# Hybrid decoder layer: the products of the triangular inverse take all 128 columns

## The chip, the cores and the metric

The kernel runs on one core of one Trainium2 chip. The metric is the device time of one execution in microseconds (us), taken as the median of several runs.

## The reference: what is computed

One layer of a decoder trunk, in float32, on 1024 tokens of width 1024: a SwiGLU feed-forward of width 2816, a token mixer, cross-attention over 256 memory tokens, a second SwiGLU. The change lies in the token mixer's first half, RWKV-7:

```python
def step(state, xs):
    r_t, w_t, k_t, v_t, kk_t, b_t = xs
    sa = jnp.einsum('bhvk,bhk->bhv', state, -kk_t)
    state = (state * w_t[:, :, None, :] + sa[..., None] * b_t[:, :, None, :]
             + v_t[..., None] * k_t[:, :, None, :])
    return state, jnp.einsum('bhvk,bhk->bhv', state, r_t)
```

There are 8 heads of width 64. The kernel doesn't walk over the tokens: for each segment of 128 tokens and each head it needs the inverse of a unit lower triangular 128x128 matrix, I + A, where A holds the products of the segment's keys below the diagonal.

## The kernel before

**Stages.** Feed-forward 1, the projections, the mixer (about 1120 to 1740 us of the span), the merge, the attention, feed-forward 2. In the mixer a loop of eight passes (`iteration(i, ...)`, i = 0 to 7, one for each segment) is written out by hand on every engine. Each engine runs its own list in order, and semaphores named after the steps (`W3`, `Wc3`, ...) tie them together.

**The inverse.** It is built by doubling blocks, in six levels n = 1 to 6 with blocks of b = 2^n. `Ur` holds the transposed inverse of the blocks so far for all 8 heads (128 x 8 x 128), `Tr` the inverse not transposed, `AL` the part of A that joins two blocks at this level. One level is this chain:

- TensorE, step W: 8 products (one for each head) of `AL` and `Ur` into PSUM tile g1. The 64 columns used are the odd blocks of `Ur`; the others are left out, so that 8 x 64 columns fill one PSUM bank.
- ScalarE, step Wc (L1450): copies g1 to `Wr`. Behind it, from level 2 on, step Tc (L1458) brings the last level's new half of the inverse into `Tr`, from a transpose made by VectorE (steps T, L1932) or, for the last two levels, by TensorE (step V: `Ur` times an identity into g2).
- TensorE, step E: 8 products of `Tr` and `Wr` into g0. It waits for Tc, at level 1 for Wc.
- VectorE, step U (L1928): subtracts g0 from the odd blocks of `Ur`. The next W waits for it, and for GpSimd's `AL` of its level (L691).

**What lies between.** TensorE fills the waits with other work in a fixed order: the products of the mLSTM half of the mixer, and pieces of the projection of the merge gates (`fill`, L884: 128x512 products of `hq` and `gw`), in slots of a set number (`gates("a4")` stands between W and E of level 4, `gates("b4")` behind E). The slots are the same in passes 1, 2, 4, 5, 6 and 7; pass 3 has none from `a4` on, pass 0 has more of them early.

```python
early = dict(s1=3, s2=2, s3=5, s4=4, s5=4, s6=6)
middle = dict(s7=5, a1=6, b1=4, b2=4, b3=5)
late = dict(a4=4, b4=5, a5=3, b5=4, a6=2, b6=4, F=2)
```

GpSimd makes `AL` of level 4 only after it has finished the output of the pass before (`Ys`, `yo`).

Of the kernel before, what the change touches and what calls it, by code (L numbers as in the profile page):

```python
# [15 lines left out]
P = 128  # L16
# [3 lines left out]
HALF = 512  # L20
# [8 lines left out]
HD = 64  # L29
# [10 lines left out]
LEVELS = 7  # L40
# [11 lines left out]
ACT = mybir.ActivationFunctionType  # L52
F32 = mybir.dt.float32
# [78 lines left out]
def layer_kernel(nc, a, out):  # L132
# [90 lines left out]
    idr = place("mix", "small", "idr", [P, P], F32R)  # L223
# [9 lines left out]
    Ur, Tr = (mix(n, (P, NH, SEG), F32R) for n in ("Ur", "Tr"))  # L233
    levels_at = top["mix"]
    Wr = mix("Wr", (P, NH, SEG), F32R)
# [3 lines left out]
    AL = mix("AL", (P, 2, NH, SEG), F32R)  # L239
# [70 lines left out]
    def flat(ap):  # L310
        return ap.rearrange("p a b -> p (a b)")

    def blocks(ap, n, odd):

        return ap.rearrange("p (q two b) -> p q two b", two=2, b=1 << n)[:, :, odd, :]

    def packed(ap, n):

        return ap.rearrange("p (q b) -> p q b", b=1 << n)

    def con(col, n=P, rows=P):
        return cst[0:rows, col:col + n]
# [428 lines left out]
    def _(pe):  # L751
# [148 lines left out]
        def iteration(i, front, back, more=True):  # L900
            F, B, M = f_pe, b_pe, m_pe
            j = i - 1
            g0, g1, g2, m0, m1 = G[0], G[1], G[2], G[3][:, 0, :], G[3][:, 1, :]
# [22 lines left out]

                fill(slots[min(i, NSEG)].get(slot, 0))

            def level(dst, n, left, right):

                for h in range(NH):
                    last = nc.tensor.matmul(packed(dst[:, 0, h * HD:(h + 1) * HD], n), left[:, h, :], right(h),  # L932
                                            start=True, stop=True)
                return last

            def turned(n):

                return level(g2, n, Ur, lambda h: blocks(idr[:, 0:P], n, 0)).then_inc(*F.sig(f"V{n}"))

            if front:  # L940
                gates("s1")
# [4 lines left out]
            if back:  # L946
# [4 lines left out]
                for n, e, r, rows in heads:  # L951
                    last = nc.tensor.matmul(g2[:, e, r * HD:(r + 1) * HD], W1m[rows, r, :], S0s[rows, r, :],
                                            start=False, stop=r == RC - 1, skip_group_check=True)
                last.then_inc(*B.sig("U"))
            gates("s3" if front else "x1")
            if back:
                pe.wait_ge(*b_act.at("Un", j))
                for n, e, r, rows in heads:
                    nc.tensor.matmul(g2[rows, e, r * P:(r + 1) * P], vtok[:, r, rows], Mv[:, n, :], start=r == 0,
                                     stop=False, skip_group_check=True)  # L960
                for n, e, r, rows in heads:
                    nc.tensor.matmul(g2[rows, e, r * P:(r + 1) * P], Un[:, n, :], Mu[:, n, :], start=False,
                                     stop=False, skip_group_check=True)
                for n, e, r, rows in heads:
                    last = nc.tensor.matmul(g2[rows, e, r * P:(r + 1) * P], S0s[rows, r, :], rho[rows, r, :],
                                            start=False, stop=r == RC - 1, skip_group_check=True)
# [3 lines left out]
                for n, e, r, rows in heads:  # L970
                    nc.tensor.matmul(g1[rows, 1, r * HD:(r + 1) * HD], ktok[:, r, rows], vtok[:, r, rows],
                                     start=r == 0, stop=False, skip_group_check=True)
                for n, e, r, rows in heads:
                    last = nc.tensor.matmul(g1[rows, 1, r * HD:(r + 1) * HD], btok[:, r, rows], Un[:, n, :],
                                            start=False, stop=r == RC - 1, skip_group_check=True)
                last.then_inc(*B.sig("dS"))
            if front:
# [9 lines left out]
                                 stop=True).then_inc(*F.sig("bonus"))  # L987
# [44 lines left out]
            for n in range(1, LEVELS):  # L1032
                pe.wait_ge(*f_dve.at(f"U{n - 1}", i))
                pe.wait_ge(*f_pool.at(f"am{n}", i))
                level(g1, n, AL[:, n % 2], lambda h: blocks(Ur[:, h, :], n, 1)).then_inc(*F.sig(f"W{n}"))
                if n == 1:
                    gates("a1")
                    pe.wait_ge(*f_pool.at("T0", i))
                    pe.wait_ge(*f_dve.at("B", i))
                elif n - 1 > SMALL:  # L1040
                    pe.wait_ge(*f_dve.at("Mv", i))
                    turned(n - 1)
                if n == 2:
                    pe.wait_ge(*m_dve.at("qe", i))
                    nc.tensor.matmul(m0, con(C_ONES), flat(Pb[:]), start=True, stop=False)
                    for h in range(MH):
                        last = nc.tensor.matmul(m0[:, h * SEG:(h + 1) * SEG], CN[:, 1, h, :], qe[:, h, :],
                                                start=False, stop=h == MH - 1)
                    last.then_inc(*M.sig("den"))
                if n == 3:  # L1050
                    pe.wait_ge(*m_act.at("aden", i))
                    for h in range(MH):
                        dst = m0[:, h * SEG:(h + 1) * SEG]
                        nc.tensor.matmul(dst, mvtok[:, h, :], Pb[:, h, :], start=True, stop=False)
                        last = nc.tensor.matmul(dst, CN[:, 0, h, :], qe[:, h, :], start=False, stop=True)
                    last.then_inc(*M.sig("num"))
                if n == 5:
                    pe.wait_ge(*m_dve.at("hm", i))
                    nc.tensor.matmul(m0, con(C_ONES), flat(hm[:]), start=True, stop=True).then_inc(*M.sig("mean"))
                if n == 6:  # L1060
                    pe.wait_ge(*m_pool.at("ysq", i))
                    nc.tensor.matmul(m0, con(C_ONES), flat(mysq[:]), start=True, stop=True).then_inc(*M.sig("var"))
                if n > 1:
                    gates(f"a{n}")
                pe.wait_ge(*f_act.at(f"Wc{n}" if n == 1 else f"Tc{n - 1}", i))
                level(g0, n, Tr, lambda h: packed(flat(Wr[:])[:, h * HD:(h + 1) * HD], n)).then_inc(*F.sig(f"E{n}"))
                if n == 1:
                    pe.wait_ge(*b_dve.at("ve", j))
                    gram(kap, rho, g2).then_inc(*F.sig("Mv"))
                gates(f"b{n}")  # L1070
# [12 lines left out]
            for n, e, r, rows in heads:  # L1083
                last = nc.tensor.matmul(g2[rows, 1, r * P:(r + 1) * P], atok[:, r, rows], Uf[:, n, :],
                                        start=True, stop=True)
# [142 lines left out]
    def _(act):  # L1228
# [166 lines left out]
        def iteration(i, front, back, more=True):  # L1395
# [51 lines left out]
                return  # L1447
            for n in range(1, LEVELS):
                act.wait_ge(*f_pe.at(f"W{n}", i))
                activation(flat(Wr[:])[:, 0:HALF], g1[:, 0, :], ACT.Copy).then_inc(*F.sig(f"Wc{n}"))  # L1450
                if n > 1:
                    if n - 1 > SMALL:
                        act.wait_ge(*f_pe.at(f"V{n - 1}", i))
                        src = packed(g2[:, 0, :], n - 1)
                    else:
                        act.wait_ge(*f_dve.at(f"T{n - 1}", i))
                        src = blocks(flat(Uf[:]), n - 1, 0)
                    activation(blocks(flat(Tr[:]), n - 1, 0), src, ACT.Copy).then_inc(*F.sig(f"Tc{n - 1}"))  # L1458
                if n == 2:
                    act.wait_ge(*m_pe.at("den", i))  # L1460
                    activation(flat(aden[:]), m0, ACT.Abs).then_inc(*M.sig("aden"))
# [4 lines left out]
            if more:  # L1466
                nc.scalar.preload_act_table(ACT.Tanh)
            act.wait_ge(*f_pe.at(f"V{LEVELS - 1}", i))
            activation(blocks(flat(Tr[:]), LEVELS - 1, 0), packed(g2[:, 0, :], LEVELS - 1),
                       ACT.Copy).then_inc(*F.sig(f"Tc{LEVELS - 1}"))  # L1470
            if more:
                ahead(i + 1, gate=False)
# [157 lines left out]
    def _(dve):  # L1630
# [181 lines left out]
        def iteration(i, front, back):  # L1812
# [103 lines left out]
            for n in range(1, LEVELS):  # L1916
                if n == 3:
                    dve.wait_ge(*m_act.at("aden", i))
                    tt(aden[:], aden[:], nmb[:], ALU.max).then_inc(*M.sig("dmax"))
                    dve.wait_ge(*M.at("dmax", i))  # L1920
                    nc.vector.reciprocal(aden[:, 0:2], aden[:, 0:2]).then_inc(*M.sig("rec0"))
                if n == 4:
                    nc.vector.reciprocal(aden[:, 2:MH], aden[:, 2:MH]).then_inc(*M.sig("rec"))
                    dve.wait_ge(*M.at("rec", i))
                    dve.wait_ge(*m_pe.at("num", i))
                    tt(flat(hm[:]), m0, flat(aden[:]), ALU.mult).then_inc(*M.sig("hm"))
                dve.wait_ge(*f_pe.at(f"E{n}", i))
                tt(blocks(flat(Ur[:]), n, 1), blocks(flat(Ur[:]).bitcast(F32), n, 1), packed(g0[:, 0, :], n),  # L1928
                   ALU.subtract).then_inc(*F.sig(f"U{n}"))
                if n <= SMALL:  # L1930
                    dve.wait_ge(*F.at(f"U{n}", i))
                    nc.vector.transpose(flat(Uf[:]), flat(Ur[:]).bitcast(F32)).then_inc(*F.sig(f"T{n}"))  # L1932
                if n == 1:
                    dve.wait_ge(*b_dve.at("S", j))
                    dve.wait_ge(*f_pe.at("Mv", i))
                    tt(S0s[:], St[:], Pi[:, :, 0:1].to_broadcast([P, RC, HD]), ALU.mult).then_inc(*F.sig("S0s"))
                    gram("Mv", Mv, g2, C_UPEQ)
                    if back:
                        output_norm()
                if n == 3:  # L1940
                    gate_half(1)
                if n == 5:
                    dve.wait_ge(*m_pe.at("mean", i))
                    stt(flat(hm[:]), m0, -1.0 / P, flat(hm[:]), ALU.mult, ALU.add).then_inc(*M.sig("yc"))
# [251 lines left out]
```

## Time and profile before

| | |
|---|---|
| median of 3 runs | 2991.3 us (2990.96 to 2994.0) |
| time of the profiled execution | 3002.78 us |
| its span, first to last instruction | 3001.0 us |
| TensorE busy | 2877.7 us, 96% |
| VectorE, ScalarE, GpSimd busy | 1353.9, 544.8, 1246.4 us |
| mean granted TensorE clock | 0.975 of full speed |

Full speed is 2.4 GHz, and the profile knows one lower level, 1.2 GHz (0.50). The profile shows TensorE's weight loads (PEld) apart from its products (PE), and a busy PE is not PE at its peak: a product of few columns counts as busy while the next weights are loaded. What matters for a wait in the mixer is whether TensorE stands still for it.

### The profile page before, as it was taken

To read this page: it belongs to the slowest core of one execution; us is meant where nothing else is said; L and a number is where in the kernel's file an instruction comes from. 1 tells how busy PE (TensorE), PEld (TensorE's weight loads), DVE (VectorE), ACT (ScalarE), POOL (GpSimd) and SP (SyncE) were. 2 spreads that over 40 slices of the span, in tenths; PEclk is the share of its full clock that TensorE was granted. 3 is DMA by queue.
4 is the path that set the end of the run, shared out by engine and by line. 5 is a ranking of instruction groups with operands and counts; after the bars stand their busy time and mean duration, and the time that the engine had idled before them with its cause. 6 is when DMAs were issued, how large, how long until landed. Compare 5 with 4: busy or idle time off the path is not lost.

```text
span 3001.0 us, 36791 instructions
## 1 busy us (share of the span) xinstructions
PE 2877.7 (96%) x14694; PEld 2387.5 (80%) x14694; DVE 1353.9 (45%) x1109; ACT 544.8 (18%) x793; POOL 1246.4 (42%) x627
## 2 busy tenths in 40 slices
PE   7999999999999979999999999998899999999996
PEld 6888888888788867777877778888788888888885
DVE  5431331235557525666776645443354321331334
ACT  3100000002001112333433322214311100000011
POOL 3444333334794623555554533331044333334432
PEclk9999999999999999988998999999999999999998
DMA  3111111112862643324442254113011111111111
GB/s 133 47 45 48 49 49 49 49 44 104 320 226 98 233 151 129 94 85 151 99 103 89 82 200 161 49 56 126 0 49 42 49 49 49 49 49 49 49 40 72
DMA packets 115401, 271.35 MB, mean 90 GB/s; under 512 B 7644, under 2 KB 58972, under 8 KB 108272
## 3 DMA queue, kind: packets, MB, share of 16 engines
q1 hardware_dynamic: 93504, 210.79, 21.7%
q10 hardware_dynamic: 21808, 59.27, 5.2%
q8 instruction: 68, 1.11, 0.2%
q14 instruction: 21, 0.17, 0.0%
HBM read 207.56 MB, written 62.44 MB: 90 GB/s over the span
## 4 chain that ended last, share of the span: by engine, by line
PE 78%; issue 9%; POOL 6%; DVE 4%; ACT 1%; DMA 0%; SPq 0%; ACTq 0%; POOLq 0%; DVEq 0%
PE G L760 23%; PE G L762 23%; PE G L761 23%; PE G L884 2%; POOL AL L691 2%; PE G L932 1%; PE G L1173 1%; POOL Tr L685 1%; ACT sx L1567 0%; DVE nt_a L1652 0%; DVE px L2024 0%; DVE mx L2016 0%; POOL rho L674 0%; PE G L1165 0%; SPq L559 0%
## 5 line engine op out<-in xcount | busy, mean ns | idle before, releaser
L724 POOL TENSOR_TENSOR whi<-raw,zero 128x1024 fp32r<-128x1024 f32 (+1 forms) x199 | 378.2, 1900 | 1313.0 <-PE G L762 1233.1
L760 PE MATMUL G<-hhi,whi 128*128 128x512 f32 x2032 | 794.6, 391 | 19.6 <-DVE hlo L1658 16.4
L761 PE MATMUL G<-hlo,whi 128*128 128x512 f32 x2032 | 792.6, 390 | 0.0
L762 PE MATMUL G<-hhi,wlo 128*128 128x512 f32 x2032 | 792.4, 390 | 0.0
L727 POOL TENSOR_TENSOR wlo<-raw,whi 128x1024 fp32r<-128x1024 f32 (+1 forms) x199 | 482.5, 2425 | 15.6
L760 PEld LDWEIGHTS G<-hhi,whi 128*128 128x128 f32 x2032 | 382.7, 188 | 102.5 <-issue 13.1
L761 PEld LDWEIGHTS G<-hlo,whi 128*128 128x128 f32 x2032 | 382.7, 188 | 80.0 <-issue 0.7
L762 PEld LDWEIGHTS G<-hhi,wlo 128*128 128x128 f32 x2032 | 382.8, 188 | 79.5
L760 PE MATMUL G<-ahi,whi 128*128 128x512 f32 x960 | 374.2, 390 | 2.7 <-DVEq L461 2.7
L762 PE MATMUL G<-ahi,wlo 128*128 128x512 f32 x960 | 373.5, 389 | 0.0
L761 PE MATMUL G<-alo,whi 128*128 128x512 f32 x960 | 373.5, 389 | 0.0
L884 PE MATMUL G<-hq,gw 128*128 128x512 f32 x768 | 237.6, 444 | 21.9 <-DVE ev L1810 20.4
L760 PEld LDWEIGHTS G<-ahi,whi 128*128 128x128 f32 x960 | 180.2, 188 | 40.4 <-issue 3.1
L761 PEld LDWEIGHTS G<-alo,whi 128*128 128x128 f32 x960 | 180.2, 188 | 37.5 <-issue 0.2
L762 PEld LDWEIGHTS G<-ahi,wlo 128*128 128x128 f32 x960 | 180.2, 188 | 37.5
L884 PEld LDWEIGHTS G<-hq,gw 128*128 128x128 f32 x768 | 145.4, 203 | 64.5 <-issue 40.1
L1304 ACT ACTIVATE s<-s 128x1024 f32<-128x1024 f32 x44 | 46.7, 1061 | 759.9 <-DVE s L1731 759.9
L1689 DVE SCALAR_TENSOR_TENSOR xT<-G,xT 128x1024 f32 x32 | 39.2, 1225 | 292.2 <-PE G L762 292.2
L1731 DVE TENSOR_TENSOR s<-G,nrx 128x1024 f32<-128x1024 f32 x44 | 53.9, 1225 | 245.8 <-PE G L762 244.9
L1737 DVE TENSOR_TENSOR s<-s,G 128x1024 f32<-128x1024 f32 x44 | 53.8, 1222 | 224.6 <-PE G L762 224.0
L1733 DVE TENSOR_TENSOR s<-s,nrx 128x1024 f32<-128x1024 f32 x44 | 132.6, 3014 | 49.6 <-ACT s L1304 49.6
L1739 DVE TENSOR_TENSOR alo<-s,ahi 128x1024 f32 x44 | 127.5, 2897 | 59.6 <-ACT ahi L1306 59.6
(329 smaller groups left out, 3321.4 us busy)
## 6 DMA issues: line engine op xcount, KB each, us to landing
gw<-gw_d SPq DMA_DIRECT2D x32, 1024.0 KB, 5.4
raw<-in_wg SPq DMA_DIRECT2D x44, 512.0 KB, 3.3
raw<-in_wu SPq DMA_DIRECT2D x44, 512.0 KB, 3.3
raw<-in_wd SPq DMA_DIRECT2D x32, 512.0 KB, 3.3
gw_d<-gw SPq DMA_DIRECT2D x16, 1024.0 KB, 4.7
graw<-in_gates_in SPq DMA_DIRECT2D x16, 512.0 KB, 7.0
raw<-in_ml_in SPq DMA_DIRECT2D x16, 512.0 KB, 3.8
zml_d<-po ACTq DMA_DIRECT2D x16, 512.0 KB, 2.6
```

Source lines behind the costliest of these rows:

```text
L691: tt(AL[:, n % 2], Am[:], copies(C_LEV + n * P), ALU.mult).then_inc(*F.sig(f"am{n}"))
L724: nc.gpsimd.tensor_tensor(whi[:, k, 0:w], raw[:, k, 0:w], zero[:].to_broadcast([P, w]), ALU.add).then_inc(hi_made, 1)
L727: nc.gpsimd.tensor_tensor(wlo[:, k, 0:w], raw[:, k, 0:w], whi[:, k, 0:w].bitcast(F32), ALU.subtract).then_inc(split_made, 1)
L760: nc.tensor.matmul(dst, wh, hi, start=start, stop=False)
L761: nc.tensor.matmul(dst, wh, lo, start=False, stop=False)
L762: return nc.tensor.matmul(dst, wl, hi, start=False, stop=stop)
L884: last = nc.tensor.matmul(G[3][:, 1, :], gw[:, k, way == 2, t * P:(t + 1) * P], hq[:, t + (way == 1) * KD, :], start=at == 0, stop=at == 3 ...
L1304: activation(s0[:], s0[:], ACT.Silu).then_inc(f_silu, 1)
L1731: tt(s0[:], flat(bank_act(c.act + r)[:]), nrx[:], ALU.mult).then_inc(act_free, 1)
L1733: tt(s0[:], s0[:], nrx[:], ALU.mult).then_inc(f_scaled, 1)
L1737: tt(s1[:], s0[:], flat(bank_dve(c.dve + r)[:]), ALU.mult).then_inc(dve_free, 1)
L1739: tt(alo[:, i * 2 + r, :], s1[:], ahi[:, i * 2 + r, :].bitcast(F32), ALU.subtract).then_inc(a_lo, 1)
```

## The change

All three kinds of products take 128 columns for each head: W multiplies by the whole of `Ur`, E by the whole of `Wr`, V by the whole identity. Each fills two PSUM banks in place of one. The number of products stays. Step Wc copies both banks, 1024 elements of a partition in place of 512. Steps U and Tc still handle 512 elements, and now pick the blocks they need out of PSUM with a stride, where PSUM had them packed before.

```diff
-            def level(dst, n, left, right):
+            def turned(n):
 
                 for h in range(NH):
-                    last = nc.tensor.matmul(packed(dst[:, 0, h * HD:(h + 1) * HD], n), left[:, h, :], right(h),
-                                            start=True, stop=True)
-                return last
-
-            def turned(n):
-
-                return level(g2, n, Ur, lambda h: blocks(idr[:, 0:P], n, 0)).then_inc(*F.sig(f"V{n}"))
+                    last = nc.tensor.matmul(flat(g2[:])[:, h * P:(h + 1) * P], Ur[:, h, :], idr[:, 0:P], start=True,
+                                            stop=True)
+                return last.then_inc(*F.sig(f"V{n}"))
...
-                level(g1, n, AL[:, n % 2], lambda h: blocks(Ur[:, h, :], n, 1)).then_inc(*F.sig(f"W{n}"))
+                eight(g1, AL[:, n % 2], Ur).then_inc(*F.sig(f"W{n}"))
...
-                level(g0, n, Tr, lambda h: packed(flat(Wr[:])[:, h * HD:(h + 1) * HD], n)).then_inc(*F.sig(f"E{n}"))
+                eight(g0, Tr, Wr).then_inc(*F.sig(f"E{n}"))
...
-                activation(flat(Wr[:])[:, 0:HALF], g1[:, 0, :], ACT.Copy).then_inc(*F.sig(f"Wc{n}"))
+                activation(flat(Wr[:]), flat(g1[:]), ACT.Copy).then_inc(*F.sig(f"Wc{n}"))
...
-                        src = packed(g2[:, 0, :], n - 1)
+                        src = blocks(flat(g2[:]), n - 1, 0)
...
-            activation(blocks(flat(Tr[:]), LEVELS - 1, 0), packed(g2[:, 0, :], LEVELS - 1),
+            activation(blocks(flat(Tr[:]), LEVELS - 1, 0), blocks(flat(g2[:]), LEVELS - 1, 0),
...
-                tt(blocks(flat(Ur[:]), n, 1), blocks(flat(Ur[:]).bitcast(F32), n, 1), packed(g0[:, 0, :], n),
+                tt(blocks(flat(Ur[:]), n, 1), blocks(flat(Ur[:]).bitcast(F32), n, 1), blocks(flat(g0[:]), n, 1),
```

`eight` was there before:

```python
def eight(dst, left, right):
    for n in range(NH):
        last = nc.tensor.matmul(flat(dst[:])[:, n * P:(n + 1) * P], left[:, n, :], right[:, n, :],
                                start=True, stop=True)
    return last
```

## Rows read from the trace of the kernel before

**Rows 1.** The page: busy times, and the granted clock in 40 slices.

```profile
PE 2877.7 (96%) x14694; PEld 2387.5 (80%) x14694; DVE 1353.9 (45%) x1109; ACT 544.8 (18%) x793; POOL 1246.4 (42%) x627
...
PEclk9999999999999999988998999999999999999998
```

**Rows 2.** Groups by line and shape, 1150 to 1720 us: busy us, mean ns, idle before.

```profile
L932 PE MATMUL G<-Wr,Tr 128*128 128x64 f32 x384 | 56.5, 295 | 3.9 <-ACT Tr L1458 2.4 <-issue 1.5
L932 PE MATMUL G<-Ur,AL 128*128 128x64 f32 x384 | 56.1, 295 | 13.9 <-DVE Uf L1932 6.9 <-POOL AL L691 3.7 <-DVE Ur L1928 3.3
...
L1450 ACT ACTIVATE Wr<-G 128x512 fp32r<-128x512 f32 x48 | 28.7, 598 | 208.3 <-PE G L932 208.3
...
L932 PE MATMUL G<-idr,Ur 128*128 128x64 f32 x128 | 19.5, 301 | 0.0
```

**Rows 3.** Timeline of TensorE, end of pass 0: start us, length us, instructions.

```profile
1192.15 1.99 PE L921 MATMUL G<-Ur,Am 128*128 128x128 f32 x16
1193.89 1.06 PE L932 MATMUL G<-idr,Ur 128*128 128x64 f32 x8
```

**Rows 4.** ScalarE in the attention: its copy of 1024 elements out of PSUM.

```profile
L1563 ACT ACTIVATE pxt<-G 128x1024 f32<-128x1024 f32 x8 | 8.2, 1023 | 7.1 <-PE G L1165 7.1
```

**Rows 5.** Timeline of pass 4, end of level 3 and level 4.

```profile
1472.58 2.38 POOL L691 TENSOR_TENSOR AL<-Am,cst 128x1024 fp32r<-128x1024 f32 x1
...
1472.72 1.41 PE L884 MATMUL G<-hq,gw 128*128 128x512 f32 x5
...
1475.11 1.05 PE L932 MATMUL G<-Ur,AL 128*128 128x64 f32 x8 [0.98 <-DVE Uf L1932]
...
1476.00 1.18 PE L884 MATMUL G<-hq,gw 128*128 128x512 f32 x4
1476.20 0.60 ACT L1450 ACTIVATE Wr<-G 128x512 fp32r<-128x512 f32 x1 [4.84 <-PE G L932]
1476.69 0.62 ACT L1458 ACTIVATE Tr<-Uf 128x512 fp32r<-128x512 f32 x1
...
1477.37 0.85 PE L932 MATMUL G<-Wr,Tr 128*128 128x64 f32 x6 [0.19 <-ACT Tr L1458]
```

**Rows 6.** The same timeline, pass 4, level 2: Tc and E.

```profile
1465.76 0.68 ACT L1458 ACTIVATE Tr<-Uf 128x512 fp32r<-128x512 f32 x1
...
1466.82 1.06 PE L932 MATMUL G<-Wr,Tr 128*128 128x64 f32 x8
```

**Rows 7.** Timeline, pass 4, level 5: Tc and E.

```profile
1481.03 0.62 ACT L1458 ACTIVATE Tr<-Uf 128x512 fp32r<-128x512 f32 x1
...
1481.97 0.97 PE L932 MATMUL G<-Wr,Tr 128*128 128x64 f32 x8
```

**Rows 8.** Timeline of ScalarE: the first Wc of pass 4 and of pass 5.

```profile
1459.99 0.60 ACT L1450 ACTIVATE Wr<-G 128x512 fp32r<-128x512 f32 x1 [4.13 <-PE G L932]
...
1528.98 0.60 ACT L1450 ACTIVATE Wr<-G 128x512 fp32r<-128x512 f32 x1 [4.12 <-PE G L932]
```

**Rows 9.** The same: the first Wc of pass 6 and of pass 7.

```profile
1601.21 0.60 ACT L1450 ACTIVATE Wr<-G 128x512 fp32r<-128x512 f32 x1 [4.11 <-PE G L932]
...
1681.17 0.60 ACT L1450 ACTIVATE Wr<-G 128x512 fp32r<-128x512 f32 x1 [4.12 <-PE G L932]
```

**Rows 10.** Stretches with busy us of each engine, granted clock, DMA share, GB/s.

```profile
1403.90:1421.00 17.10, 15.54 (x61) 13.16 (x60) 3.57 (x5) 4.85 (x7) 6.50 (x5) 0.50 0.61 244
1547.30:1554.10 6.80, 6.80 (x20) 5.09 (x20) 1.94 (x2) 1.11 (x2) 3.22 (x2) 0.50 0.12 48
1619.00:1642.90 23.90, 23.90 (x84) 20.09 (x84) 4.83 (x7) 4.85 (x7) 8.66 (x6) 0.50 0.05 19
1460.00:1528.90 68.90, 65.53 (x535) 54.15 (x535) 51.06 (x64) 26.96 (x53) 38.80 (x25) 1.00 0.46 105
1601.20:1619.00 17.80, 16.36 (x117) 13.72 (x116) 15.80 (x18) 4.60 (x8) 12.86 (x8) 1.00 0.53 156
1165.00:1171.80 6.80, 6.80 (x25) 5.47 (x23) 2.18 (x3) 1.29 (x3) 2.35 (x1) 0.50 0.22 54
```

More of the change, by code:

```diff
@@ L315, in blocks @@
         return ap.rearrange("p (q two b) -> p q two b", two=2, b=1 << n)[:, :, odd, :]
-    def packed(ap, n):
-        return ap.rearrange("p (q b) -> p q b", b=1 << n)
     def con(col, n=P, rows=P):
```

## The prediction

> **What bounds the kernel now.** I read the page first, then the groups of the mixer, then the timeline of one level of the inverse, then the granted clock in stretches. TensorE is busy 96% of the span, and its clock is below full speed in a few slices only, most of them in the mixer [rows 1]. So time goes or comes in three ways: TensorE's own work gets longer, TensorE waits more or less for the chain W, Wc, Tc, E, U, or its clock changes. ScalarE and VectorE are mostly idle; what they do matters only where TensorE has run out of other work.
>
> The chain seldom stops TensorE. Over 48 levels its products waited 3.9 us before E and 13.9 us before W [rows 2]. Level 4 shows both: after five gate products TensorE stands about 1 us until W of level 4, since GpSimd's AL ends only at 1472.58 + 2.38 = 1474.96, and the four gate products behind W end before Tc does, so E waits another 0.19 us [rows 5].
>
> **The products: 112 groups of eight (48 W, 48 E, 16 V), from 64 to 128 columns.** The sixteen records of F, 128 columns each, take 1.99 us from the first start to the last end, eight of 64 columns take 1.06 [rows 3]: eight more in 0.93 us, 0.116 us for each. Within the 64-column group it is (1.06 - 0.30) / 7 = 0.109, taking the last one's length as 0.30 [rows 2]. Both walk at the pace of the weight loads, 128 columns for each product, which don't change. The difference of 0.007 times 896 products is 6.3 us at most; at least it is 0. The tail is the uncertain part of the subtraction, and the pace of the loads explains both numbers, so I take 0.
>
> The Trainium skill (TensorE: Matmul & The Clock Gate, Back-to-back issue gap) gives an isolated gap that grows with the columns, about 60 cycles at 64 and 134 at 128. By it the sum would rise by some 31 ns for each of 896 products, an estimate of 28 us. The rows on F and V speak against that here, because a weight load stands before every product.
>
> **Wc copies 1024 elements.** It takes 0.598 us [rows 2]; ScalarE's copy of 1024 out of PSUM takes 1.023 us [rows 4]. So each Wc ends 0.43 us later, and Tc behind it too. What hides this is the work TensorE has between W and E. Level by level, in a pass at full clock:
>
> - Level 4: Tc ends at 1476.69 + 0.62 = 1477.31, E starts at 1477.37 [rows 5]. No cover: the whole 0.43 us, in the seven passes 1 to 7 (pass 0 has cover), 3.0 us.
> - Level 5: Tc ends at 1481.65, E starts at 1481.97 [rows 7]. Of the 0.32 us some 0.05 is the way from one engine to the other, as at level 4, so 0.27 covers and 0.16 shows; in seven passes 1.1 us. In pass 3, which has no gate products there, up to 0.4 us.
> - Level 2: Tc ends at 1466.44, E starts at 1466.82 [rows 6]; 0.10 us shows. It is absorbed before W of level 4, which waits for GpSimd and not for this chain.
> - Levels 1 and 3 have more cover than level 2. At level 6 Tc waits for V behind W, and that hides Wc.
>
> The sum is +4.5 us. Everything behind U in a pass follows it, so I take nothing as given back. The bounds are 0 and 48 x 0.43 = 20.6 us, the second if nothing covered.
>
> **Strided reads from PSUM in U and Tc.** No row shows a fine stride out of PSUM. The nearest is Tc of level 1's blocks out of SBUF, two elements at a time: 0.68 us against 0.62 at wide blocks [rows 5, 6]. I take 0, as VectorE and ScalarE already step through SBUF in the same pattern; the upper bound is 0.06 x 64 = 3.8 us.
>
> **The clock.** This is the largest term. Pass 4 ran wholly at 2.4 GHz [rows 10], and from its first Wc to that of pass 5 it took 68.99 us [rows 8]. Pass 5 has the same work, contained one stretch of 6.8 us at 1.2 GHz [rows 10], and took 1601.21 - 1528.98 = 72.23 [rows 8, 9], +3.2. Pass 6 contained one of 23.9 us and took 79.96 [rows 9], +11.0. Passes 1 and 2 repeat these two almost to the digit, so there are four such stretches, 28.4 us together. Pass 3 loses its clock for 17.1 us, and pass 0 for 6.8 [rows 10].
>
> Where does it fall? Pass 4's E of level 4 starts 17.38 us after its first Wc [rows 5, 8]. The same offset gives 1546.36 in pass 5 and 1618.59 in pass 6. The clock falls at 1547.3 and 1619.0: 0.9 and 0.4 us later, right behind W, four gate products and E of level 4 with their two waits. At 1601.2 to 1619.0 it was still 1.00 [rows 10]. Passes 4 and 7 have the same place and keep the clock. So this place is marginal: a little less or more work there decides in some passes. After the change the two groups of products there, 16 in all, stream 2048 columns instead of 1024, against 2048 of the four gate products; it is a third more work between the same waits, less what 0.43 us more of waiting before E takes away. And once the clock is low, the following products are wider too, so the long stretch of pass 6 should shrink to the short one.
>
> I price it so. In the profiled execution all four stretches go, 28.4 us, and pass 0's 3.2 too, since it begins behind E of level 1 with the same products. Pass 3 keeps its own: without gate products TensorE really stands still. A remaining fall in one pass of eight or so costs 2.4 us. In this execution's own time: 3002.8 + 4.5 - 31.6 + 2.4 = 2978.
>
> The median before is 2991.3, 11.5 below this execution. I read that as fewer or shorter falls in those runs: 28.4 - 11.5 = 16.9 us are left to win, and for pass 0 on average 1. So 2991.3 + 4.5 - 16.9 - 1.0 + 2.4 = 2980.3. Were the 11.5 us a cost of profiling alone, it would be 2991.3 + 4.5 - 31.6 + 2.4 = 2967, the lower end.
>
> **The rivals.**
>
> *The clock doesn't care for columns.* The records call TensorE just as busy with 64 columns as with 128: a busy share can't tell them apart. Then only the ScalarE term stays: 2991.3 + 4.5 = 2995.8, within what can be told from no change (0.2%, 6 us, is about what a measurement of this kernel resolves). For it speaks that passes 4 and 7 keep the clock with the same work, so chance has a part; against it, that the falls stand behind the narrowest work of the pass.
>
> *Slower: the longer wait before E of level 4 pulls the clock down.* E waits 0.19 us now and would wait 0.62. If only standing still counts, passes that now keep the clock lose it. One more long stretch costs 11.0 us [rows 8, 9]: 2995.8 + 11.0 = 3007. It decides as soon as the stretches added cost over 1.5 us, which one short stretch of 3.2 us does.
>
> The Trainium skill (the same page, The HAM clock gate) says that the clock follows how busy the array has been. If busy means occupied, as the records count it, this rival follows. If it means columns streamed, my forecast does. The page doesn't say which, so it gets no more weight than the trace gives it.
>
> *Products at 128 columns cost more than weight loads hide.* At the bound of 6.3 us, plus strided reads at 3.8, the gain shrinks to about nothing: 2980.3 + 10.1 = 2990.4, no change.
>
> **How the numbers follow.** Falls at level 4 mostly vanish: 0.64, 2980, own range 2970 to 2988. Clock unmoved: 0.17, 2996. Products and reads at their bounds: 0.08, 2990. Slower by the clock: 0.11, 3007. The range 2967 to 2997 reaches from profiling as the whole difference to the unmoved clock and leaves out the slower rival and tails, somewhat under 2 in 10. Faster than 2985.3: nearly all of the first case and a little of the third, 0.65. Within 0.2%: 0.22. Slower than 2997.3: 0.13.
>
> **What would show each step.** Right: the 896 products keep a mean near 280 to 295 ns, eight of them still take about 1.06 us; Wc takes 1.02 us; E of level 4 starts 0.43 us later after W than now; U stays at 0.68 us; passes 1, 2, 5 and 6 take 69.5 to 70 us from first Wc to first Wc, and the stretches at 0.50 between 1225 and 1700 us are down to pass 3's and perhaps a short one. Wrong: if passes without a low stretch take over 71 us, the ScalarE or product term was too small. If the low stretches are as many and as long as before, the clock doesn't follow columns. If pass 4 or 7 has one, the second rival holds. If the median falls by less than 6 us though the stretches are gone, the runs before had fewer of them than the difference of 11.5 us made me think.

## The result and the profile after

The changed kernel takes 2977.85 us (median of 5 runs, 2975.95 to 2980.32) against 2994.0 for the kernel before in the same rounds (5 runs, 2990.96 to 2999.85): a ratio of 0.9944, with a 95% interval of 0.9931 to 0.9957. Its profiled execution took 2978.5 us over a span of 2976.7.

The page of the changed kernel, busy times and granted clock, against [rows 1]:

```profile
PE 2850.4 (96%) x14694; PEld 2361.4 (79%) x14694; DVE 1354.5 (46%) x1109; ACT 564.4 (19%) x793; POOL 1247.0 (42%) x627
...
PEclk9999999999999999998999999999999999999998
```

TensorE is busy 27.3 us less, though 896 of its products became twice as wide. ScalarE is busy 19.6 us more. The clock row has one slice under 9 inside the mixer, where it had three.

The groups of the mixer after, 1150 to 1700 us (busy us, mean ns, idle before), against [rows 2]:

```profile
L917 PE MATMUL G<-Wr,Tr 128*128 128x128 f32 x384 | 55.0, 288 | 7.3 <-ACT Tr L1450 5.6 <-DVE Bm L1817 1.5
L917 PE MATMUL G<-Ur,AL 128*128 128x128 f32 x384 | 52.5, 281 | 12.6 <-DVE Uf L1924 6.6 <-POOL AL L687 3.7 <-DVE Ur L1920 1.6
...
L1442 ACT ACTIVATE Wr<-G 128x1024 fp32r<-128x1024 f32 x48 | 49.2, 1025 | 182.2 <-PE G L917 182.2
L1920 DVE TENSOR_TENSOR Ur<-Ur,G 128x512 fp32r<-128x512 f32 x48 | 32.5, 678 | 80.1 <-PE G L917 80.1
...
L928 PE MATMUL G<-idr,Ur 128*128 128x128 f32 x128 | 18.0, 286 | 0.0
```

The wide products have a lower mean (281 to 288 ns) than the narrow ones had (295 to 301), because fewer of them ran at the low clock: in pass 4, at full clock in both kernels, the narrow ones have a mean of 272 to 277 ns and the wide ones 275 to 277. Wc takes 1.025 us. The subtraction U, which now reads PSUM with a stride, takes 0.678 us. Before E, TensorE waits 7.3 us in all in place of 3.9; of it 5.6 are for Tc, where it was 2.4.

Level 4 of pass 4 in the timeline of the changed kernel, against [rows 5]:

```profile
1457.85 2.38 POOL L687 TENSOR_TENSOR AL<-Am,cst 128x1024 fp32r<-128x1024 f32 x1
...
1458.07 1.36 PE L880 MATMUL G<-hq,gw 128*128 128x512 f32 x5
...
1460.38 1.08 PE L917 MATMUL G<-Ur,AL 128*128 128x128 f32 x8 [0.95 <-DVE Uf L1924]
...
1461.29 1.14 PE L880 MATMUL G<-hq,gw 128*128 128x512 f32 x4
1461.49 1.03 ACT L1442 ACTIVATE Wr<-G 128x1024 fp32r<-128x1024 f32 x1 [4.42 <-PE G L917]
...
1462.42 0.62 ACT L1450 ACTIVATE Tr<-Uf 128x512 fp32r<-128x512 f32 x1
...
1463.09 1.11 PE L917 MATMUL G<-Wr,Tr 128*128 128x128 f32 x8 [0.66 <-ACT Tr L1450]
```

From W to E it is 2.71 us in place of 2.26: the 0.43 us of the longer copy and little else. W itself takes 1.08 us for eight products of 128 columns, where it took 1.05 for eight of 64.

The first Wc of passes 4 to 7 in the timeline of ScalarE, against [rows 8, 9]:

```profile
1445.20 1.03 ACT L1442 ACTIVATE Wr<-G 128x1024 fp32r<-128x1024 f32 x1 [4.14 <-PE G L917]
...
1515.07 1.03 ACT L1442 ACTIVATE Wr<-G 128x1024 fp32r<-128x1024 f32 x1 [4.16 <-PE G L917]
...
1584.97 1.03 ACT L1442 ACTIVATE Wr<-G 128x1024 fp32r<-128x1024 f32 x1 [4.14 <-PE G L917]
...
1654.84 1.03 ACT L1442 ACTIVATE Wr<-G 128x1024 fp32r<-128x1024 f32 x1 [4.15 <-PE G L917]
```

The differences are 69.87, 69.90 and 69.87 us, where they were 68.99, 72.23 and 79.96. A pass at full clock has become 0.88 us longer, and now all of them but pass 3 are at full clock. The stretches of the changed kernel (columns as in [rows 10]):

```profile
1225.00:1386.60 161.60, 151.35 (x1210) 124.38 (x1208) 121.99 (x147) 65.12 (x115) 94.73 (x58) 1.00 0.44 112
1386.60:1407.10 20.50, 17.53 (x65) 14.54 (x66) 5.35 (x8) 6.02 (x9) 8.20 (x5) 0.50 0.65 256
1407.20:1690.30 283.10, 266.70 (x2156) 219.05 (x2155) 206.06 (x253) 117.55 (x213) 155.15 (x96) 1.00 0.33 93
1690.40:1700.60 10.20, 10.01 (x54) 9.68 (x55) 4.10 (x7) 1.79 (x3) 3.31 (x3) 0.50 0.41 145
```

Between 1225 and 1690 us only pass 3's stretch, 20.5 us, is left at half clock. The stretch at 1690.4 stands at the end of the mixer, behind level 6 of pass 7; the kernel before has one of 6.8 us there, at 1718.0, so the change doesn't remove it.

### The profile page after: what moved, and what is told of

It is laid out like the page before. It is cut to its first block, busy times and chain, and to the rows that moved or that the text cites. A ratio compares the mean times of both kernels' runs of the same rounds, so it can differ in the third digit from the quotient of the medians.

```text
span 2976.7 us, 36791 instructions
## 1 busy us (share of the span) xinstructions
PE 2850.4 (96%) x14694; PEld 2361.4 (79%) x14694; DVE 1354.5 (46%) x1109; ACT 564.4 (19%) x793; POOL 1247.0 (42%) x627
## 4 chain that ended last, share of the span: by engine, by line
PE 78%; issue 9%; POOL 6%; DVE 4%; ACT 1%; DMA 1%; SPq 0%; POOLq 0%; ACTq 0%; DVEq 0%
PE G L756 24%; PE G L758 24%; PE G L757 24%; PE G L880 2%; POOL AL L687 2%; PE G L1165 1%; PE G L917 1%; POOL Tr L681 1%; ACT sx L1559 0%; DVE nt_a L1644 0%; DVE px L2016 0%; DVE mx L2008 0%; POOL rho L670 0%; PE G L1157 0%; SPq L555 0%
## 5 line engine op out<-in xcount | busy, mean ns | idle before, releaser
L880 PE MATMUL G<-hq,gw 128*128 128x512 f32 x768 | 221.7, 421 | 22.2 <-DVE ev L1802 20.5
L880 PEld LDWEIGHTS G<-hq,gw 128*128 128x128 f32 x768 | 137.8, 192 | 60.1 <-issue 37.0
L1681 DVE SCALAR_TENSOR_TENSOR xT<-G,xT 128x1024 f32 x32 | 39.2, 1225 | 292.2 <-PE G L758 292.2
L1723 DVE TENSOR_TENSOR s<-G,nrx 128x1024 f32<-128x1024 f32 x44 | 53.9, 1225 | 245.8 <-PE G L758 244.9
```

Of the source, the lines that this page charges most:

```text
L880: last = nc.tensor.matmul(G[3][:, 1, :], gw[:, k, way == 2, t * P:(t + 1) * P], hq[:, t + (way == 1) * KD, :], start=at == 0, stop=at == 3 ...
L1723: tt(s0[:], flat(bank_act(c.act + r)[:]), nrx[:], ALU.mult).then_inc(act_free, 1)
```

## Experiments

The main theory is that the gain is the clock, kept up where the wider products stream more columns, and the price is ScalarE's longer copy. The main rivals: the gain comes from the shift in time that the longer copy makes, and waits alone decide over the clock. The kernel before ran beside each group: 2991.8 us in 23 runs beside the first four, 2991.9 in 12 beside the others. "A pass" is the distance between the first Wc of two passes in the profiled execution; "low" counts the stretches at half clock that begin around E of level 4, in the six passes that have gate products there (1, 2, 4, 5, 6 and 7).

| kernel | median us | ratio to before (95% interval) | pass at full clock | low |
|---|---|---|---|---|
| before | 2991.8 | | 68.99 | 4 of 6 |
| changed, again | 2976.9 | 0.9942 (0.9923 to 0.9962) | 69.87 | 0 |
| only W wide | 2969.4 | 0.9922 (0.9901 to 0.9943) | 69.02 | 0 |
| all wide, copy of 512 | 2970.4 | 0.9924 (0.9902 to 0.9945) | 69.14 | 0 |
| all narrow, copy of 1024 | 3005.5 | 1.0046 (1.0028 to 1.0065) | 69.69 | 3 of 6 |
| changed, a4 behind E | 2993.2 | 1.0003 (0.9990 to 1.0016) | none | 6 of 6 |
| all narrow, six gate products in a4 | 2971.5 | 0.9930 (0.9908 to 0.9952) | 68.87 | 0 |
| only E wide | 2971.5 | 0.9935 (0.9909 to 0.9961) | 69.21 | 2 of 6 |
| only W wide, pass 3 filled | 2965.6 | 0.9909 (0.9887 to 0.9930) | 69.02 | 0 |

The profiled execution of the first result has 0 of 6 as well. So at this place the two kernels with narrow products and four gate products before E fell in 7 of 12 passes. The seven executions with more columns there (the changed kernel twice, the four other variants with wide products and four gate products before E, and the narrow one with six) fell in 2 of 42.

### Only W at 128 columns

```diff
-                level(g1, n, AL[:, n % 2], lambda h: blocks(Ur[:, h, :], n, 1)).then_inc(*F.sig(f"W{n}"))
+                eight(g1, AL[:, n % 2], Ur).then_inc(*F.sig(f"W{n}"))
...
-                activation(flat(Wr[:])[:, 0:HALF], g1[:, 0, :], ACT.Copy).then_inc(*F.sig(f"Wc{n}"))
+                activation(packed(flat(Wr[:])[:, 0:HALF], n), blocks(flat(g1[:]), n, 1), ACT.Copy).then_inc(*F.sig(f"Wc{n}"))
```

> The kernel before, with only step W at 128 columns; ScalarE picks the 512 odd elements of a partition out of PSUM with a stride, E and V stay at 64 columns. Half of the added columns, no longer copy. If the clock is kept by the columns streamed behind the wait of level 4, most low stretches of passes 1, 2, 5, 6 go, none of the ScalarE cost (0.88 us a pass in the changed kernel) comes, and it takes 2970 to 2980 us. If the columns are not the cause, it stays at the kernel before, 2990 to 3000, low stretches included. If a strided read out of PSUM costs 0.06 us each or more, passes at full clock take over 69.4 us in place of 69.0.

It took 2969.4 us, 22 below the kernel before and just under the range. The stretches of its trace, and its Wc:

```profile
1225.00:1385.80 160.80, 150.74 (x1217) 125.11 (x1216) 122.85 (x149) 59.51 (x116) 95.68 (x58) 1.00 0.42 115
1385.80:1406.30 20.50, 18.16 (x72) 15.64 (x72) 5.58 (x8) 4.85 (x7) 9.09 (x6) 0.50 0.60 241
1406.40:1686.00 279.60, 263.60 (x2147) 218.12 (x2146) 205.61 (x253) 107.86 (x212) 153.72 (x94) 1.00 0.36 94
...
L1450 ACT ACTIVATE Wr<-G 128x512 fp32r<-128x512 f32 x48 | 28.7, 598 | 190.9 <-PE G L921 190.9
```

A full-clock pass is as long as before (69.02 against 68.99), so there is no gain in the work itself: the same count of instructions, and at level 4 the same waits (1.01 and 0.22 us in pass 4). Pass 6 took 70.81 us without a low stretch, since TensorE stood 1.6 us once before E of level 1 with no release that the profile shows; that is no part of the change. The columns of the 48 groups of W differ, and with them the order in which W reads `Ur` and writes PSUM; the low stretches of passes 1, 2, 5 and 6 are gone. Wc takes 598 ns with the strided read from PSUM, exactly as without it.

### All products wide, ScalarE copies only what is needed

```diff
-                activation(flat(Wr[:]), flat(g1[:]), ACT.Copy).then_inc(*F.sig(f"Wc{n}"))
+                if n == 1:
+                    activation(flat(Wr[:]), flat(g1[:]), ACT.Copy).then_inc(*F.sig(f"Wc{n}"))
+                else:
+                    activation(blocks(flat(Wr[:]), n, 1), blocks(flat(g1[:]), n, 1),
+                               ACT.Copy).then_inc(*F.sig(f"Wc{n}"))
```

> The changed kernel, but from level 2 on ScalarE copies only the odd blocks, 512 elements of a partition, in place; the other columns of Wr keep old numbers that no later step uses. All products at 128 columns, the copy back at about 0.60 us. If the columns hold the clock and the longer copy is the cost, passes at full clock take 69.0 to 69.3 us in place of 69.87, low stretches as few as in the changed kernel, and the time is 5 to 7 us below it: 2971 to 2973. If the longer copy itself had a part in the gain (by moving the passes against the chip's clock control), it is above the changed kernel: 2980 to 2995.

It took 2970.4 us, just under the range and 7.5 below the changed kernel's first result (6.5 below its repeat), and a pass is 69.14 us against its 69.87. So 0.73 of the 0.88 us a pass is the copy, and 0.15 is left for the wider products and the rest, the long copy of level 1 among it. Its two forms of Wc:

```profile
L1445 ACT ACTIVATE Wr<-G 128x512 fp32r<-128x512 f32 x40 | 23.9, 598 | 151.2 <-PE G L917 151.2
L1443 ACT ACTIVATE Wr<-G 128x1024 fp32r<-128x1024 f32 x8 | 8.2, 1029 | 37.4 <-PE G L917 37.4
```

### Only the longer copy, products at 64 columns

```diff
-                activation(flat(Wr[:])[:, 0:HALF], g1[:, 0, :], ACT.Copy).then_inc(*F.sig(f"Wc{n}"))
+                activation(flat(Wr[:]), flat(g1[:]), ACT.Copy).then_inc(*F.sig(f"Wc{n}"))
```

> The kernel before with 64-column products, where only ScalarE's copy Wc takes 1024 elements, the second half being numbers that nothing uses. It has the cost and not the columns. If the columns hold the clock: low stretches as in the kernel before or more, passes at full clock near 69.6 to 69.9 us, and 4 to 15 us slower than before: 2998 to 3009. If the gain came from the longer copy's shift of the passes in time, it is as fast as the changed kernel, 2975 to 2985.

It took 3005.5 us (12 runs, 2995.2 to 3014.8), 13.7 above the kernel before. That the copy's shift in time makes the gain is ruled out. A full-clock pass is 69.69 us, +0.70, or 4.9 us in seven passes. The other 8.8 us I put down to the clock, and the runs agree: their mean clock was 0.971 to 0.978, that of the kernel before beside them 0.975 to 0.982. The profiled execution's level 4 in pass 1, and two of its low stretches:

```profile
1247.03 1.05 PE L932 MATMUL G<-Ur,AL 128*128 128x64 f32 x8 [0.97 <-DVE Uf L1932]
...
1247.91 1.18 PE L884 MATMUL G<-hq,gw 128*128 128x512 f32 x4
1248.11 1.03 ACT L1450 ACTIVATE Wr<-G 128x1024 fp32r<-128x1024 f32 x1 [4.42 <-PE G L932]
...
1249.71 1.91 PE L932 MATMUL G<-Wr,Tr 128*128 128x64 f32 x8 [0.62 <-ACT Tr L1458]
...
1249.60:1273.50 23.90, 23.79 (x81) 19.99 (x82) 4.88 (x7) 5.76 (x8) 8.00 (x5) 0.50 0.06 21
...
1618.20:1625.00 6.80, 6.80 (x21) 5.09 (x21) 2.36 (x3) 1.54 (x2) 2.74 (x2) 0.50 0.15 57
```

The waits (0.97 and 0.62 us) are those of the changed kernel (0.95 and 0.66), the gate products too. Here the clock falls at this very place, 0.1 us before E starts; there it doesn't. Falls came in passes 1, 6 and 7. The copy alone doesn't decide each time: passes 2, 4 and 5 of this execution kept the clock.

### The gate products of a4 moved behind E

```diff
-        late = dict(a4=4, b4=5, a5=3, b5=4, a6=2, b6=4, F=2)
+        late = dict(a4=0, b4=9, a5=3, b5=4, a6=2, b6=4, F=2)
```

> The changed kernel with the four gate products between W and E of level 4 moved behind E (slot a4 from 4 to 0, b4 from 5 to 9). TensorE then stands still for some 1.5 us before E, in each of the passes 0 to 7 that has late slots. By the waits alone it costs about 0.9 us a pass, 6.5 us: 2984. If this place with its work and waits decides over the clock, the low stretches come back in most passes, 3.2 to 11 us each: 3000 to 3040. If the place has nothing to do with it, 2984.

It took 2993.2 us, 15 to 16 above the changed kernel, so all of its gain is lost. Every pass now has a low stretch. Two of its windows, and level 4 of pass 4:

```profile
1249.90:1253.30 3.40, 3.40 (x10) 2.78 (x10) 1.93 (x2) 0.00 (x0) 2.68 (x2) 0.54 0.08 31
1321.60:1328.40 6.80, 6.80 (x26) 5.93 (x25) 1.94 (x2) 0.00 (x0) 3.33 (x2) 0.52 0.16 60
...
1466.22 1.08 PE L917 MATMUL G<-Ur,AL 128*128 128x128 f32 x8 [0.96 <-DVE Uf L1924]
1468.93 1.97 PE L917 MATMUL G<-Wr,Tr 128*128 128x128 f32 x8 [1.63 <-ACT Tr L1450]
```

The stretches are short (3.4 and 6.8 us, and 13.7 in pass 3, which has no gate products there). Nine gate products follow at once; that they shorten the stretches is likely, but not shown. The direction was as expected; the size was below the 3000 to 3040 I gave, since I had priced in long stretches. No pass ran at full clock, so waits and clock can't be split here.

### The marginal place filled another way: six gate products before E, all products narrow

```diff
-        late = dict(a4=4, b4=5, a5=3, b5=4, a6=2, b6=4, F=2)
+        late = dict(a4=6, b4=3, a5=3, b5=4, a6=2, b6=4, F=2)
```

> The kernel before, all products at 64 columns, with two of the gate products behind E of level 4 moved in front of it (slot a4 from 4 to 6, b4 from 5 to 3). At the marginal place this adds 1024 columns, as many as the change does, by another way. If the columns streamed there decide, the low stretches of the passes mostly go though no product is wider, at a cost of about 0.2 us a pass: 2973 to 2983. If the width of the products itself is what matters, it stays at 2990 to 2996.

2971.5 us, just under the range: the kernel before with two numbers of a table changed is faster than the changed kernel. Its passes take 68.87 us, since the wait before E of level 4 is filled, and its stretches are:

```profile
1225.00:1383.00 158.00, 148.66 (x1204) 123.23 (x1202) 120.39 (x146) 58.59 (x114) 93.17 (x57) 1.00 0.40 114
1383.20:1403.60 20.40, 17.92 (x71) 15.40 (x71) 5.33 (x8) 4.94 (x8) 8.82 (x6) 0.51 0.63 253
1406.70:1410.10 3.40, 3.40 (x31) 2.85 (x27) 3.30 (x5) 2.34 (x9) 0.00 (x0) 0.51 0.02 5
1410.60:1683.00 272.40, 259.02 (x2099) 214.11 (x2098) 199.93 (x247) 104.09 (x200) 153.49 (x94) 1.00 0.35 96
```

Both low stretches are pass 3's; the kernel before has the same pair, 17.1 us at 1403.9 and 3.4 at 1424.4.

So the width of the products isn't needed. The pass has no column more than before, two gate products only stand in front of E and not behind it; so the place counts. This run can't take apart how much the columns do and how much the filled wait of 0.19 us. The first experiment keeps that wait and loses the stretches too, but changes the order of W's reads and writes, which this one leaves as it was. What both have in common is more columns at this place.

### Only E at 128 columns

```diff
-                level(g0, n, Tr, lambda h: packed(flat(Wr[:])[:, h * HD:(h + 1) * HD], n)).then_inc(*F.sig(f"E{n}"))
+                eight(g0, Tr, Wr).then_inc(*F.sig(f"E{n}"))
...
-                activation(flat(Wr[:])[:, 0:HALF], g1[:, 0, :], ACT.Copy).then_inc(*F.sig(f"Wc{n}"))
+                if n == 1:
+                    activation(blocks(flat(Wr[:]), n, 0), packed(g1[:, 0, :], n), ACT.Copy)
+                activation(blocks(flat(Wr[:]), n, 1), packed(g1[:, 0, :], n), ACT.Copy).then_inc(*F.sig(f"Wc{n}"))
...
-                tt(blocks(flat(Ur[:]), n, 1), blocks(flat(Ur[:]).bitcast(F32), n, 1), packed(g0[:, 0, :], n),
+                tt(blocks(flat(Ur[:]), n, 1), blocks(flat(Ur[:]).bitcast(F32), n, 1), blocks(flat(g0[:]), n, 1),
```

> The kernel before with only step E at 128 columns: ScalarE spreads the 512 packed elements to the odd blocks of Wr (at level 1 it fills the even ones too, one more copy), U reads PSUM with a stride, W and V stay at 64. Added columns as in the first experiment, but behind the wait. If the columns of either group serve, 2968 to 2978. If only those of W do, since the clock falls behind W and the wait for E, the low stretches stay in part: 2982 to 2995.

2971.5 us (6 runs, 2968.2 to 2984.6), as expected if either group serves. In the profiled execution it serves not quite as well as W: two short stretches of 3.4 us are left at level 4, in passes 5 and 7, where the kernel with W wide has none. That is one execution of each. The slowest run, at a clock of 0.981, may have had more:

```profile
1387.80:1404.80 17.00, 15.44 (x60) 12.95 (x59) 3.44 (x5) 4.85 (x7) 6.30 (x5) 0.50 0.60 241
1412.00:1531.00 119.00, 112.96 (x931) 92.94 (x931) 91.54 (x113) 46.87 (x89) 68.41 (x43) 1.00 0.42 108
1531.20:1534.60 3.40, 3.40 (x13) 2.92 (x13) 1.95 (x3) 0.00 (x0) 3.40 (x2) 0.52 0.27 104
1671.00:1674.40 3.40, 3.40 (x13) 2.92 (x13) 2.15 (x3) 0.00 (x0) 3.40 (x2) 0.50 0.35 135
```

### Pass 3 filled with products that nothing uses

The kernel with only W wide, and in pass 3 thirteen products on constants (the expectation says fourteen) in its empty late slots:

```diff
+                if i == GATES // 4 - 1 and slot in late:
+                    pe.wait_ge(ev_made, made[0] // (3 * KD) + 1)
+                    for _ in range((late[slot] + 1) // 2):
+                        nc.tensor.matmul(G[3][:, 1, 0:2 * P], con(C_ID), con(C_LEV, 2 * P), start=True, stop=True)
```

> The kernel of the first experiment (only W at 128 columns), and in pass 3, whose late slots are empty, half as many float32 products of 256 constant columns as other passes have gate products there; their result is used by nothing. 14 added products of about 0.43 us. If pass 3 loses its clock because TensorE streams too little there, the 20.5 us stretch at 1.2 GHz goes and pass 3 takes about 69 to 70 us in place of 75.5, so 5 to 6 us less in all: about 2964. If the clock falls there for another reason, the 14 products come on top: 2973 to 2976.

It took 2965.6 us, the fastest of all and 26 below the kernel before, with 13 products more than needed; TensorE is busy with them for 7.1 us. Pass 3 takes 68.92 us in place of 75.46. The stretch around it:

```profile
1366.00:1436.00 70.00, 66.63 (x545) 55.72 (x544) 51.30 (x63) 27.80 (x54) 39.97 (x25) 1.00 0.46 154
```

The products fill a wait as well: TensorE stands 0.29 us before E of level 4 in pass 3, where it stood 1.20. This run doesn't tell whether their columns or the shorter wait keep the clock.

### The changed kernel again

> The changed kernel again, so that it stands beside the others on the same chip: 2976 to 2980, some 15 us below the kernel before of these rounds, by every theory; a pass at full clock 69.87 us.

2976.9 us against 2991.9, ratio 0.9942, with 69.87 us for a pass at full clock: the first result repeats.

## Why the prediction was right

**The sum.** 2980 was forecast and 2977.85 measured. The change itself came out larger than forecast: 16.1 us in the rounds of the first result and 15.0 in the later ones, where 11.0 was forecast. Within the profiled executions 24.7 us were forecast and 24.3 measured. That is closer than its terms: the longer passes cost 1.7 us more than I took, and the 2.4 us kept for a remaining fall weren't needed. These two errors nearly cancel, which is luck.

**The products cost next to nothing.** Eight of 128 columns take 1.08 us where eight of 64 take 1.05, and their mean is 281 to 288 ns, as forecast. Together with all that the copy doesn't explain it is 0.15 us a pass, about 1 us in all, far under the bound of 6.3. The Trainium skill (TensorE: Matmul & The Clock Gate, Back-to-back issue gap) gives the gap that grows with the columns for isolated products. By it I had estimated 28 us, 31 ns for each product; the trace shows about 4 ns ((1.08 - 1.05) / 8), with a weight load in front of every product.

**Wc.** 1.025 us, as forecast, and E of level 4 starts 0.45 us later behind W. The sum of 0.59 us a pass (levels 4 and 5) was too small: a pass grew by 0.88, of it 0.73 by the copy, in seven passes 6.2 us, not 4.5. The term that was mis-sized is level 5. From its W to the W of level 6 pass 4 took 4.26 us before and 4.58 after, 0.32 more, where I had 0.16. I had read the cover from Tc's end to the first product of E. But what waits for Tc is the load of `Tr` as weights, and that stood 0.22 us in front of the product:

```profile
1481.75 1.09 PEld L932 LDWEIGHTS G<-Wr,Tr 128*128 128x128 f32 x8
1481.97 0.97 PE L932 MATMUL G<-Wr,Tr 128*128 128x64 f32 x8
...
1467.86 0.30 PEld L917 LDWEIGHTS G<-Wr,Tr 128*128 128x128 f32 x2 [0.47 <-ACT Tr L1450]
1467.86 0.33 PE L917 MATMUL G<-Wr,Tr 128*128 128x128 f32 x1
```

The first two lines are before, the others after. Before, the load started 0.10 us behind Tc's end (1481.65), so there was hardly any cover; after, it waits 0.47 us for Tc.

**Strided reads.** Nothing, as forecast: 0.678 us for U as before, 598 ns for the strided Wc of the first experiment.

**The clock.** The four stretches of passes 1, 2, 5 and 6 are gone, and pass 3 kept its own. I had read 17.1 us for pass 3; a stretch of 3.4 us at 1424.4 belongs to it, so it is 20.5 us before and after. That the falls at level 4 go with the columns there is shown: the kernel with narrow products and the same waits has them, and adding columns in three ways (W, E, gate products) removes all or most of them. Each way changes one thing more (the order of access, a wait), but not the same one. Why a fall comes in one pass and not in the next, with the same waits, stays open. Pass 0's stretch is also gone, but that is not shown to come from the columns. The kernel with narrow products and six gate products in a4 has none there either, and the run with W wide and pass 3 filled has one of 3.4 us.

For the median the gain from the clock was sized too small. An estimate from the runs: 15.0 or 16.1 us gained in all and 6.2 paid for the longer passes make 21 to 22 us from the clock, where 15.5 (16.9 + 1.0 - 2.4) were forecast. The first experiment, which pays nearly nothing, gains 22.

**The 11.5 us between the profiled execution and the median** I had read as fewer falls, not as profiling. The runs agree: of the 23 beside the first experiments the fastest (2980.3 us) had a mean clock of 0.981, the slowest (3000.4) 0.975, and those near the median 0.978. The kernel before spreads over 20 us, along with its mean clock; the changed kernel spreads over 4.4 us in its first five runs and 6.3 in the seven later ones.

**The rivals.** That the clock doesn't care for columns is ruled out by the first experiment together with the six gate products in a4. The slower rival is half true: with the longer wait before E and no added columns the time rises (3005.5 us with the copy alone, 8.8 more than its 4.9 us of waiting) and the mean clock sinks, and in its trace pass 7 has a fall, which had none before; the added columns outweigh it. The third, products and reads at their bounds, is ruled out by the 0.15 us a pass. The Trainium skill (the same page, The HAM clock gate) says that the clock follows how busy the array has been. By the busy time of the records alone the two kernels don't differ, 96% in both; what differs is the columns at level 4, and the count of falls with them.

## What to carry to other kernels

Here a weight load stands before every product and sets its pace, and 64 columns more cost next to nothing (1.08 us for eight in place of 1.05). In a stretch of narrow products with small waits such columns kept the clock up. Before changing the products, look for the place in front of each low stretch and move existing work there: two numbers in a table gave more here than the rewrite (2971.5 us against 2976.9). If only part of a wide result is used, copy only that part: without the long copy the gain was 21 us, with it 15. And when you ask how much cover an engine has in front of a wait, look at the weight load, not at the first product.

## What the runs showed of the hardware

- The same stretch of instructions ran at 1.2 or 2.4 GHz from one pass to the next, with the same waits at level 4 (0.98 and 0.19 us in passes 4 and 5, 1.00 and 0.19 in pass 6). What that costs a pass here is 3.2 us for a stretch of 6.8 and 11.0 for one of 23.9.
- A mean busy share doesn't show the risk: it is 96% before and after. With narrow products the clock fell at level 4 in 7 of 12 passes, with more columns at that place in 2 of 42.
- ScalarE and VectorE read PSUM in every second block of 2 to 64 elements at the speed of packed reads: 598 and 678 ns for 512 elements of a partition.
- A wait for a stationary operand ends at its weight load. At level 5 the load stood 0.22 us in front of the first product, and so 0.22 us less was covered than the products show.
- Thirteen products on constants, for which TensorE is busy 7.1 us and which nobody needs, made the kernel faster by about 4 us (2969.4 to 2965.6, run in different rounds), since pass 3 kept its clock.
